# Global attention: keys in two halves, probabilities times values as three bf16 products

## The reference, cut to what matters

```
def one_block(qi):
    logits = jnp.einsum('bqkgd,bskd->bkgqs', qi, k, preferred_element_type=jnp.float32)
    p = jax.nn.softmax(logits, axis=-1)
    return jnp.einsum('bkgqs,bskd->bqkgd', p.astype(v.dtype), v)
```

## Time and profile before

| | |
|---|---|
| median of 3 runs | 2337.54 us (2336.62 to 2340.11) |
| the profiled execution's own time | 2339.17 us |
| its span, first to last instruction | 2337.3 us |
| TensorE, matmuls | 2267.6 us busy (97%), 23919 instructions |
| VectorE | 1618.8 us (69%) |
| ScalarE | 1224.1 us (52%) |
| GpSimd | 1090.9 us (47%) |
| granted TensorE clock, mean | 0.991 |
| global attention, wide items | from about 244 to 435 us of the span |
| banded attention | from about 430 to 537 us |
| experts | from about 800 us to the end |

### The profile page before, as it was taken

One profiled execution on the slowest core, in us unless ns is written; L12 is line 12 of the kernel. 1 busy time (PEld: TensorE's weight loads), 2 busy tenths in 40 slices (PEclk: granted clock), 3 DMA queues, 4 the chain that ended last, 5 costly groups with the idle time before them and its releaser, 6 DMA issues.

```text
span 2337.3 us, 55038 instructions
## 1 busy us (share of the span) xinstructions
PE 2267.6 (97%) x23919; PEld 1664.6 (71%) x24026; DVE 1618.8 (69%) x1973; ACT 1224.1 (52%) x1568; POOL 1090.9 (47%) x711
## 2 busy tenths in 40 slices
PE   8998999999999999989999999999999999999996
PEld 3554676664444458688888888888888888888874
DVE  4776666583222456777877878788878878787875
ACT  4333666593111236556655665665566555656554
POOL 0000111132332215556666677667667766766742
PEclk9999999999999999999999999999999999999998
DMA  9102201503222345578899999989998998999996
GB/s 340 40 22 73 55 2 38 181 2 91 55 54 63 103 159 163 185 278 288 303 334 341 316 338 329 324 316 342 331 320 319 340 336 308 342 335 320 323 326 239
DMA packets 252439, 524.24 MB, mean 224 GB/s; under 512 B 8411, under 2 KB 57676, under 8 KB 252076
## 3 DMA queue, kind: packets, MB, share of 16 engines
q1 hardware_dynamic: 241692, 488.51, 59.5%
q0 software_dynamic: 10512, 32.25, 4.7%
HBM read 492.42 MB, written 28.31 MB: 223 GB/s over the span
## 4 chain that ended last, share of the span: by engine, by line
PE 84%; DMA 4%; DVE 3%; POOL 3%; issue 3%; ACT 2%; SPq 0%; DVEq 0%; POOLq 0%; ACTq 0%
PE ps L1858 23%; PE ps L1859 22%; PE ps L1857 22%; PE ps L2041 3%; PE ps L2253 3%; PE ps L2053 3%; PE ps L1918 3%; DMA acc_sample<-arena,sidx_s 2%; PE ps L1953 1%; DVE arena L1392 1%; ACT arena L1087 1%; DMA arena<-w_in 1%; PE ps L1991 1%; POOL spare L837 1%; ACT arena L974 1%
## 5 line engine op out<-in xcount | busy, mean ns | idle before, releaser
L1858 PE MATMUL ps<-arena 128*128 128x160 bf16 (+4 forms) x5617 | 1390.5, 267 | 9.0 <-issue 3.2
L1859 PE MATMUL ps<-arena 128*128 128x160 bf16 (+4 forms) x5620 | 1391.6, 267 | 0.4
L1857 PE MATMUL ps<-arena 128*128 128x160 bf16 (+4 forms) x5528 | 1357.2, 265 | 9.2 <-POOL arena L858 5.3
L1392 DVE TENSOR_TENSOR arena<-arena 128x2048 bf16<-128x2048 f32 x379 | 912.0, 2410 | 219.9 <-ACT arena L974 215.1
L974 ACT ACTIVATE arena<-arena 128x2048 bf16<-128x2048 f32 x384 | 727.1, 1905 | 227.9 <-PE ps L1859 178.6
L1857 PEld LDWEIGHTS ps<-arena 128*128 128x128 bf16 x5624 | 550.7, 98 | 160.3 <-issue 21.0
L1859 PEld LDWEIGHTS ps<-arena 128*128 128x128 bf16 x5624 | 550.7, 98 | 154.8 <-issue 2.5
L1858 PEld LDWEIGHTS ps<-arena 128*128 128x128 bf16 x5624 | 550.7, 98 | 140.6 <-issue 0.3
L868 POOL TENSOR_TENSOR arena<-arena 128x320 bf16<-128x320 f32 x128 | 258.7, 2021 | 10.0
L865 POOL TENSOR_TENSOR arena<-arena,ones 128x320 bf16<-128x320 f32 x128 | 185.8, 1452 | 142.3 <-DVE arena L1735 142.0
L1245 ACT ACTIVATE arena<-ps 128x160 f32<-128x160 f32 x256 | 77.9, 304 | 295.4 <-PE ps L1859 295.3
(11 more groups left out here) (263 smaller groups left out, 2213.8 us busy)
## 6 DMA issues: line engine op xcount, KB each, us to landing
arena<-w_e_gate SPq DMA_DIRECT2D x64, 2048.0 KB, 9.1
arena<-w_e_up SPq DMA_DIRECT2D x64, 2048.0 KB, 9.8
arena<-w_e_down SPq DMA_DIRECT2D x64, 2048.0 KB, 9.9
arena<-w_ada SPq DMA_DIRECT2D x12, 2048.0 KB, 9.3
arena<-w_in SPq DMA_DIRECT2D x30, 512.0 KB, 5.3
arena<-x_sample SPq DMA_DIRECT2D x16, 512.0 KB, 3.7
arena<-w_in SPq DMA_DIRECT2D x3, 2048.0 KB, 16.9
arena<-w_out SPq DMA_DIRECT2D x2, 2048.0 KB, 9.2
```

Of the source, the lines that this page charges most:

```text
L1392: ve.tensor_tensor(lo, stage_half(kind, a), hi, ALU.subtract).then_inc(lo_done, 1)
L1857: pe.matmul(out, w_hi, x_hi, start=start, stop=False)
L1858: pe.matmul(out, w_hi, x_lo, start=False, stop=False)
L1859: return pe.matmul(out, w_lo, x_hi, start=False, stop=stop)
```

## The change

Three things are done together.

The scores of a wide item are made in two halves of the keys, both heads of keys 0 to 511 first (banks 0 and 1), then both heads of keys 512 to 1023 (banks 2 and 3). The first half waits for `first_exp` (the previous item's exponentials over the first 512 keys) alone, the second for `e_done`. MX becomes one reduction over both heads' first halves, and for each head a reduction over its second half and a minimum of the two negated maxima. EX becomes four exponentials of 512 keys, first halves ahead, with the sums in `den_half` and `den`, which are added before the reciprocal. Pieces are numbered the other way round: n of 0 and 1 are the first halves of the two heads (copied by ScalarE), 2 and 3 the second halves (VectorE).

The products with values become three bf16 products: values are split in step G by GpSimd into `VA` (high and low part), the upper two bytes of each float32 probability are read in place as the high part (`upper`, a view with a step of two bf16 elements), and the low part is `PTs` minus that, written as bf16 to `PL`: three of an item's four pieces by GpSimd, the fourth by VectorE (`low_vec`); for narrow items both by GpSimd. PV waits for all of them.

`PL` takes the place where `mw_load(0)` puts its data, so this load is moved: from ahead of the last six loads of `w_ada` to between them (behind c of 9), with a wait for the last product of the global branch.

```diff
         halved = len(parts) == 4 and i < first_b
+        if halved:
+            s += [("S", i, 0)] + parts[:2] + copies[:2] + [("S", i, 1), ("MX", i)]
...
-        V = at(23552, 2, NT, P)
+        VA, VB = half_words(23552, NT, 2 * P), at(24832, NT, P)
...
+        PU, PL = half_words(37376, 4, 8, 2 * P), half_words(26112, 4, 8, P)
...
-            return (n // 2, 4 * (n % 2)) if n_parts(items[i]) == 4 else (n, 0)
+            return (n % 2, 4 * (n // 2)) if n_parts(items[i]) == 4 else (n, 0)
...
-            return len(items[i][3]) > 4 and piece(i, n)[0] == 0
+            return len(items[i][3]) > 4 and piece(i, n)[1] > 0
...
+        def upper(i, hh, z):
+
+            return PU[:, i % 2 * 2 + hh, z, 1::2]
+
+        def low_vec(i, n):
+            return n_parts(items[i]) == 4 and n == 3
...
-            mw_load(0)
...
+                if c == 9:
+
+                    sp.wait_ge(pv_done, first_b)
+                    mw_load(0)
...
+                    gp.tensor_tensor(VA[:, t, 0:P], raw[:, 640:768], ones[:], ALU.mult).then_inc(v_high, 1)
+                    gp.wait_ge(v_high, t + 1)
+                    gp.tensor_tensor(VA[:, t, P:2 * P], raw[:, 640:768], VA[:, t, 0:P], ALU.subtract).then_inc(v_split, 1)
+                if k == "TE" and items[s[1]][0] == 0 and not low_vec(*s[1:]):
...
+                    gp.tensor_tensor(PL[:, i % 2 * 2 + hh, z], PTs[0][:, i % 2, hh, z], upper(i, hh, z), ALU.subtract)\
+                        .then_inc(p_low[1], 1)
...
+                    if w > 512:
+                        for h, (d, done) in enumerate(((den_half, first_exp), (den, e_done))):
+                            for hh in range(2):
+                                ac.wait_ge(nm_ready, 2 * i + hh + 1)
+                                ac.activation(probs(i, hh)[:, 512 * h:512 * h + 512], ps[:, 2 * h + hh], ACT.Exp,
+                                              bias=nm[:, i % 4, hh:hh + 1],
+                                              accum_out=d[:, i // NPAIR % 3, 2 * j + hh:2 * j + hh + 1]).then_inc(done, 1)
...
+                        ve.wait_ge(s_done, 2 * i + 1)
+                        ve.tensor_reduce(nm_half[:, 0], ps[:, 0:2], AX.X, ALU.max, negate=True).then_inc(max_half, 1)
+                        ve.wait_ge(s_done, 2 * i + 2)
+                        for hh in range(2):
+                            ve.tensor_reduce(nm_half[:, 1, hh:hh + 1], ps[:, 2 + hh], AX.X, ALU.max, negate=True)                                .then_inc(max_half, 1)
+                            ve.wait_ge(max_half, n + hh + 2)
+                            ve.tensor_tensor(nm[:, i % 4, hh:hh + 1], nm_half[:, 0, hh:hh + 1], nm_half[:, 1, hh:hh + 1],
+                                             ALU.min).then_inc(nm_ready, 1)
...
+                        h = s[2]
+                        if h == 0 and i > wide_at:
+                            pe.wait_ge(first_exp, 2 * (i - wide_at))
+                        else:
                             pe.wait_ge(e_done, 2 * i)
...
+                        scores(i, [ps[:, 2 * h + hh] for hh in range(2)], k0 + 512 * h, 512, True, (0, 1))
...
+                        passes = ((0, 0), (1, 0), (0, 1)) if br == 0 else ((0, 0),)
+                        for x, (u, v) in enumerate(passes):
+                            for hh in range(2):
+                                d = slice(u * P + hh * 64, u * P + hh * 64 + 64)
+                                if br:
+                                    w, m = VB[:, kt, d], PTs[1][:, i % 2, hh, n, :]
+                                else:
+                                    w, m = VA[:, kt, d], PL[:, i % 2 * 2 + hh, n] if v else upper(i, hh, n)
```

More of the change, by code:

```diff
@@ L141, in plan_steps @@
         done = i - (4 if i <= first_b + 4 else 5)
+        sums = []
         if done >= 0 and done % NPAIR == 0 and done < len(items) and (done < first_b) == (i <= first_b + 4):
-            s.append(("RB", done // NPAIR))
+            sums = [("RB", done // NPAIR)]
+        if not (len(parts) == 4 and i < first_b):
+            s += sums
+        halved = len(parts) == 4 and i < first_b
+        if halved:
+            s += [("S", i, 0)] + parts[:2] + copies[:2] + [("S", i, 1), ("MX", i)]
         early = 2 if len(parts) == 4 else 0
-        s += parts[:early] + copies[:early]
-        if i < len(items):
-            s += [("S", i), ("MX", i)]
+        if not halved:
+            s += parts[:early] + copies[:early]
+            if i < len(items):
+                s += [("S", i, h) for h in range(2 if wide[i] else 1)] + [("MX", i)]
         if i in (1, 3):
@@ L154, in plan_steps @@
             s_ac += 1
-        s += parts[early:3]
-        s += copies[early:3] if early else copies
+        if halved:
+            s += parts[2:3] + copies[2:3] + parts[3:] + copies[3:]
+        else:
+            s += parts[early:3]
+            s += copies[early:3] if early else copies
         v = values() if pv < len(items) and pv <= (t - 2 if parts else t - 1) else []
@@ L165, in plan_steps @@
             pv += 1
-        s += parts[3:] + (copies[3:] if early else [])
+        if not halved:
+            s += parts[3:] + (copies[3:] if early else [])
         for g in range(pv // NPAIR):
@@ L524, in encoder @@
         first_b = next(i for i, x in enumerate(items) if x[0] == 1)
+        wide_at = next(i for i, x in enumerate(items) if len(x[3]) > 4)
         def window(i):
@@ L564, in encoder @@
         n_add = lambda i: i - first_b + 1
+        freed = {}
+        uses = [0, 0, 0]
+        for n, (s, _) in enumerate(jobs):
+            if s[0] == "br":
+                freed[n] = (brow_ready, s[1] + 1)
+            elif s[0] == "AR":
+                freed[n] = (modrow_ready, s[1] + 1)
+            elif s[0] == "AC":
+                freed[n] = (mod_ready, s[1] + 1)
+            elif s[0] == "GT":
+                freed[n] = (gt_ready, s[1] + 1)
+            elif s[0] == "OT":
+                freed[n] = (rb_copied, s[1] + 1)
+            elif s[0] in ("IS", "I"):
+                freed[n] = (idx_ready, jobs[n][1] + (1 if s[0] == "IS" else 3))
+            else:
+                uses[n % 3] += 1
+                freed[n] = (t_free[n % 3], uses[n % 3])
+        def upper(i, hh, z):
+            return PU[:, i % 2 * 2 + hh, z, 1::2]
+        def low_vec(i, n):
+            return n_parts(items[i]) == 4 and n == 3
+        lows, low_at = [0, 0], {}
+        for x in steps:
+            if x[0] == "TE" and items[x[1]][0] == 0:
+                q = 0 if low_vec(*x[1:]) else 1
+                lows[q] += 1
+                low_at[x[1:]] = (p_low[q], lows[q])
         block = ctx.enter_context(nc.Block())
@@ L1077, in _ @@
                     w = len(kts) * P
-                    for hh in range(2):
+                    if w > 512:
[5 more added lines that the diff above has]
+                                              accum_out=d[:, i // NPAIR % 3, 2 * j + hh:2 * j + hh + 1]).then_inc(done, 1)
+                    for hh in range(0 if w > 512 else 2):
                         ac.wait_ge(nm_ready, 2 * i + hh + 1)
@@ L1910, in heads_turned, with scores @@
                 ins.then_inc(t_done, 1)
-            def scores(i, out, k0, w, last):
+            def scores(i, out, k0, w, last, incs=(1, 1)):
                 br, j, qt, _ = items[i]
@@ L1919, in scores @@
                                         start=n == 0, stop=n == 2, tile_position=(64 * hh, 0))
[L1920 removed]
+                        if last and n == 2 and incs[hh]:
                             ins.then_inc(s_done, 1)
@@ L2037, in _ @@
                     hh, a = piece(i, n)
-                    pe.wait_ge(e_done, 2 * i + hh + 1)
+                    if len(items[i][3]) > 4 and a == 0:
+                        pe.wait_ge(first_exp, 2 * (i - wide_at) + hh + 1)
+                    else:
+                        pe.wait_ge(e_done, 2 * i + hh + 1)
                     b = bank(s)
```

85 lines of the change are left out of this document (45 added, 40 removed).

## The result

The changed kernel was slower. Its first four executions took 2361.56 us in the median (2353.51 to 2367.5), against 2338.3 for the kernel before (four runs): a ratio of 1.0097, with a 95% interval of 1.0066 to 1.0129. Measured again later, in five executions against nine, it took 2351.83 (2350.48 to 2354.44) against 2337.63, a ratio of 1.0064 (1.0050 to 1.0078). In both the whole interval lies above 1.

What follows compares the result with a forecast made beforehand. A loop of 5.24 us through VectorE and ScalarE was to bind wide items, just above TensorE's 5.05. -4.6 - 0.6 - 0.8 + 2.4 + 1.5 + 0.5 = -1.6 from 2337.54 gave 2335.9 us, range 2327 to 2356.

Steps and rivals of the forecast that it cites:

- 0.53 us of slack: VectorE's first-half maximum is over at 2.1 of the next loop, needed at 2.63; low part and minimum cost nothing.
- VectorE and GpSimd get into each other's way: Rival, wide items: VectorE's subtraction waits for GpSimd's, next maxima 0.63 late, +17.0 us, 2352.9; chance 0.17.
- TensorE's work: Per wide item: scores 1.50, transposes 2.05, PV 1.49, sum 5.05 us, 0.30 less than now.
- the third rival: Products get no cheaper: PV 2.77 and TensorE 6.33 us an item, +29 us, 2365; chance 0.10.
- The loop: Wide items: scores, transposes, maxima, minimum, exponentials and back to TensorE take 5.24 us, longer than TensorE's 5.05.
- The first rival: TensorE stays the bound: a wide item takes 5.05 us, -5.1 us more, 2330.8; chance 0.31.
- NM's place: Ahead of the next maxima on VectorE: costs 0.97 us a group, same as present, so a group takes 21.93.
- The hand-over: Start of wide items: item 5's low parts stand behind NM on GpSimd, delaying item 8's scores: +2.4 us.
- item 8 to 9: Between these items' scores: first maxima start early, so 5.15 us becomes 4.55: -0.6.
- The end of the wide items: Z waits for the last second-half exponential; banded scores come 6.85 behind item 39's, were 5.34: +1.5 us.
- The moved load: SyncE's issuing, over 7 us, delays the last w_ada loads with 2.3 us to spare: +0.5, between 0 and 3.
- the first gains: From item 8's scores to item 9's, by first maxima that start early: -0.6 us.

Runs made afterwards that it cites:

- e_min: Changed kernel with each minimum of two numbers written as a reduction over one SBUF input: 2336.86 us, ratio 0.9999.
- e_low: Changed kernel with VectorE's low part reading its first input from the PSUM bank of the transposes: 2353.57 us, ratio 1.0070.
- e_halves: Changed kernel with the halves alone: float32 products as before, no low parts, load at its old place: 2340.09 us, ratio 1.0016.
- e_all: Changed kernel with one-input minima, VectorE's low part from PSUM, merge's load behind w_ada, NM(0) behind items 5 and 6's low parts: 2328.55 us, ratio 0.9962.
- e_min_mw_nm: e_min_mw with GpSimd's two operations of NM(0) behind the low parts of items 5 and 6: 2332.65 us, ratio 0.9983.
- after_again: The changed kernel, unaltered, measured again in five executions: 2351.83 us, ratio 1.0064.
- e_min_mw: e_min with the merge's first load behind the last of w_ada in SyncE's queue: 2334.16 us, ratio 0.9994.

## Why the prediction was wrong, point by point

**The step that failed** is "0.53 us of slack, by which I cost low part and minimum at nothing beyond the loop", with the 0.17 us for a minimum in the loop itself. The minimum took 0.416 us on average, and the first one of an item 0.61 to 0.84 in three items of four; in the fourth the low part took the wait, 1.54. The minimum stands in the loop twice, not in the slack. One wait of 0.6 us an item makes 5.24 into 5.84, which is what the timeline shows. The forecast gave 171.1 for items 9 to 39; with that one wait out (e_min) they took 171.56, with it 185.52.

**The right mechanism was among the rivals, with 0.17.** "VectorE and GpSimd get into each other's way" named VectorE's subtraction as what waits and priced it at 27 x 0.63, 2352.9 in all; the later measurement is 2351.8. But the agreement is in part luck, as the place was wrong for three items of four: e_low removed the wait of the subtraction, and nothing was gained. The minimum, a two-input operation on one number per partition, was nowhere on my list of what could wait. I had looked at GpSimd's 2.73 us as a matter of long operations, when an operation of 0.16 us waited as well.

The rows show the rule: operations with two SBUF inputs wait for GpSimd's running operation (0.74 against 0.16, 1.29 against 0.69), those with an input from PSUM or a reduction over one SBUF input don't (1213, 680, 692 and 155 ns, with GpSimd as busy). The Trainium skill, SBUF — State Buffer, section Who interferes with whom, states it so: a VectorE instruction with two SBUF inputs contends with a GpSimd instruction that reads SBUF, the contention is an exclusive lock in which the order of issue decides who blocks, and a reduction never contends on this chip. By this rule, the trace agrees for the minima and low parts shown here (0.74, ending 0.01 behind GpSimd's, and 0.155 as a reduction).

**TensorE's work** was right. PV took 1.50, forecast 1.49, so the third rival (2.77) is out. The rule that the prediction gave with it from the Trainium skill, TensorE: Matmul & The Clock Gate, Part 3, The mechanism, that weight loads overlap running matmuls only where the row group differs, is not what was measured here: all 48 loads of PV, 0.108 us each, lie within 1.41 us in the changed kernel, beside the matmuls, and the measurement decides. TensorE's 5.05 cannot be seen alone, since something else binds in every kernel; e_halves binds by TensorE at 5.45, which is the same sum with 1.90 for PV.

**The loop** of 5.24 was right to 0.07: items of e_min and e_all that have nothing else in them take 5.17 to 5.18. The first rival (TensorE bound at 5.05) was not reached. NM's place costs more than I took where VectorE's low part also waits: a group of e_min takes 22.20, forecast 21.93, and 21.60 in e_all. GpSimd's low part was forecast at 1.16 and takes 1.04.

**The hand-over** was right: +2.4 forecast, +2.3 measured to item 8, held by GpSimd as said. I had item 8 to 9 0.6 shorter; 4.52 in e_min_mw_nm, forecast 4.55, shows that step right too, but in the changed kernel the wait was followed by scores at half the clock, 2.26 us for 1.47, which takes it back.

**The end of the wide items**: the banded scores were forecast 6.85 behind item 39's and come at 6.88 in e_min. It is 7.53 in the changed kernel, and since e_min differs only in the minima, the 0.65 between them are theirs.

**The moved load** was mis-sized: +0.5, bounds 0 and 3. The banded stretch shows 3.3 to 3.7, and 2.7 less without it (e_min to e_min_mw); 2.33 to 2.61 of it is TensorE waiting for `w_ada` (2.36 in e_min), and most of the rest the lower clock behind the wait (the 16 matmuls took 3.43 and 3.49 us instead of 1.92). I had 2.3 us to spare there and put SyncE's issue at over 7; between 437.78 and 445.77 it took 8.0 in e_min, and the `w_ada` loads came behind.

```profile
437.78 0.37 SPq L658 DMA_DIRECT2D arena<-w_in  x1
...
441.13 4.60 SPq L660 DMA_DIRECT2D arena<-w_branch_b  x2
445.77 3.67 SPq L681 DMA_DIRECT2D arena<-w_ada  x2
```

In sum: -1.6 was forecast. With the items at +9.8 (instead of -4.6), the first gains at most +0.4 (instead of -0.6), the hand-over +2.3, the end +2.2 (instead of 1.5) and the banded stretch +3.3 (instead of 0.5 - 0.8), it comes to 18; the rest of the span was 4.3 shorter in after_again than in the profile before, and its start up to item 7 0.9, which makes the 12.7 between the two spans. The medians differ by 14.2.

## What to carry to other kernels

Before two engines are made to work beside each other, list every VectorE instruction with two SBUF inputs, the tiny ones first, and ask which of them stands in a loop: each can have to wait for a GpSimd operation that is running, whatever its own size (up to 0.69 us for a minimum of 0.16 here). Often it can be written with one SBUF input, as a reduction over a pair or with the other input still in PSUM. And where a saved wait gives nothing, as in e_low, look for the next wait that ends at the same event before calling the cost absent: the same edit gave 2.6 us once the first wait was gone.

## What the runs showed of the hardware that was not expected

The collision in the first profile of the changed kernel, VectorE and GpSimd, among the experts' first steps:

```profile
993.50 1.04 POOL L808 DMA_INDIRECT arena<-xn_sample,gidx_s  x1 [0.57 <-POOL gidx_s L896]
...
993.81 9.94 DVE L1715 TENSOR_TENSOR arena<-arena 128x1024 f32<-128x1024 f32 x1
...
994.55 8.11 POOL L821 TENSOR_TENSOR arena<-arena 128x2048 bf16<-128x2048 f32 x2
```

and the same place in e_low:

```profile
994.66 1.04 POOL L808 DMA_INDIRECT arena<-xn_sample,gidx_s  x1 [0.58 <-POOL gidx_s L896]
...
994.96 1.23 DVE L1715 TENSOR_TENSOR arena<-arena 128x1024 f32<-128x1024 f32 x1
...
995.71 8.89 POOL L821 TENSOR_TENSOR arena<-arena 128x2048 bf16<-128x2048 f32 x2
```

The starts relative to each other are equal to a few hundredths (0.31 and 0.30, then 0.74 and 0.75). In the one VectorE ends 1.1 us behind GpSimd's second operation, in the other it goes first and GpSimd's pair is 0.8 longer. So which of the two goes first is not settled by the recorded starts, and why it came out differently stays open. The Trainium skill, SBUF — State Buffer, section Who interferes with whom, has it that the order of issue decides who blocks; e_low's rows agree, the first profile's recorded starts don't, as they show VectorE's 0.74 ahead. VectorE found no gap between GpSimd's two successive operations here. That is no rule: the minimum at 288.04 of the same profile ended at 288.40, behind the first (288.38) of three successive low parts that went on to 290.37. The addition has two SBUF inputs, 0.75 us before a GpSimd operation of 4 us, in the kernel before as well; that it could cost 9 us there too is an inference.

The granted clock fell behind some short waits of TensorE, and not behind others. In the changed kernel it was 0.50 of full, 1.2 GHz, from 248 to 251 us, after the wait of 2.31 that ended at 246.87. An AR step of the banded stretch shows that it is no fixed price: after the same wait it took 3.31 us in e_min_mw (the 16 matmuls at 443.35, behind 1.47 of waiting) and 1.92 in e_all, here:

```profile
435.79 1.92 PE L2030 MATMUL ps<-arena,cS 128*32 128x512 f32 x16 [1.48 <-DVE modT L1493]
```

Some 1.4 us of a difference between two single profiles may be no more than that.
